# Latent attention: which engine copies the turned tiles out of PSUM

## The reference, cut to what matters

```python
s = (einsum('bqhd,bkhd->bhqk', qn_b, k_nope) + einsum('bqhd,bkd->bhqk', qr_b, k_rope)) * scale
s = where(causal, s, -inf)
p = softmax(s, axis=-1)
o = einsum('bhqk,bkhd->bqhd', p, v)
```

## Time and profile before

| | |
|---|---|
| median of 3 runs | 2243.24 us (2241.24 to 2244.13) |
| the profiled execution | 2243.0 us, of which the span from first to last instruction is 2241.2 us |
| mean granted TensorE clock | 0.957 of full |
| busy: PE, PEld | 2107.5 us (94%), 1801.6 us (80%) |
| busy: DVE, ACT, POOL | 830.4 (37%), 740.2 (33%), 776.8 us (35%) |
| chain that ended last | PE 86%, issue 4%, DVE 4%, ACT 2% |

### The profile page before, as it was taken

How to read it: one execution, slowest core, us unless ns; L and a number is a source line. 1 busy time by engine, 2 the same in 40 slices (tenths; PEclk the granted TensorE clock), 3 DMA queues, 4 the chain that set the end, 5 groups by cost and what they waited for, 6 DMA issues and landing times.

```text
span 2241.2 us, 32733 instructions
## 1 busy us (share of the span) xinstructions
PE 2107.5 (94%) x14312; PEld 1801.6 (80%) x14312; DVE 830.4 (37%) x1293; ACT 740.2 (33%) x1093; POOL 776.8 (35%) x244
## 2 busy tenths in 40 slices
PE   7999999979988889999999789989999899999998
PEld 5898888859766679999998677977777688888886
DVE  3400674053456643211222411654445554211222
ACT  5332223245546433221223243322111433221222
POOL 4443333444321344334433200343222444434432
PEclk9999999989989999999999777989999999999999
DMA  4222212222301122223224000211111422323322
GB/s 163 94 95 90 71 66 76 94 66 89 97 22 38 38 76 76 86 80 100 95 71 119 28 30 1 63 57 40 59 40 48 143 94 93 94 85 104 94 77 73
DMA packets 170982, 169.47 MB, mean 76 GB/s; under 512 B 16844, under 2 KB 164680, under 8 KB 170840
## 3 DMA queue, kind: packets, MB, share of 16 engines
q1 hardware_dynamic: 169436, 165.15, 23.4%
q10 hardware_dynamic: 1404, 2.23, 0.3%
HBM read 162.12 MB, written 5.24 MB: 75 GB/s over the span
## 4 chain that ended last, share of the span: by engine, by line
PE 86%; issue 4%; DVE 4%; ACT 2%; POOL 2%; DMA 1%; ACTq 0%; SPq 0%; DVEq 0%; POOLq 0%
PE ps L1927 84%; PE ps L1929 2%; POOL w_lo L687 1%; POOL residual L710 1%; ACT w_hi L812 0%; ACT diag L840 0%; DMA x_rows<-in_x 0%; POOL stat L704 0%; DVE sumsq L1263 0%; DVE tmp L1694 0%; DVE mla_out_lo L1882 0%; POOL gdn_small L759 0%; POOL gdn_small L757 0%; DVE gdn_on L1873 0%; DVE mla_k L1620 0%
## 5 line engine op out<-in xcount | busy, mean ns | idle before, releaser
L687 POOL TENSOR_TENSOR w_lo<-w_raw,w_hi 128x2048 fp32r<-128x2048 f32 (+3 forms) x157 | 675.4, 4305 | 903.8 <-ACT w_hi L812 903.8
L1927 PE MATMUL ps<-u_hi,w_hi 128*128 128x512 f32 (+1 forms) x1904 | 597.1, 353 | 32.5 <-DVE sg L1466 12.3
L1927 PE MATMUL ps<-u_lo,w_hi 128*128 128x512 f32 (+1 forms) x1904 | 587.3, 348 | 0.0
L1927 PE MATMUL ps<-u_hi,w_lo 128*128 128x512 f32 (+1 forms) x1904 | 586.0, 348 | 0.0
L1927 PEld LDWEIGHTS ps<-u_hi,w_hi 128*128 128x128 f32 x1904 | 335.6, 192 | 82.3 <-issue 20.6
L1927 PEld LDWEIGHTS ps<-u_hi,w_lo 128*128 128x128 f32 x1904 | 334.3, 192 | 43.2 <-issue 0.7
L1927 PEld LDWEIGHTS ps<-u_lo,w_hi 128*128 128x128 f32 x1904 | 334.7, 192 | 39.9 <-issue 1.2
L812 ACT ACTIVATE w_hi<-w_raw 128x2048 fp32r<-128x2048 f32 (+3 forms) x157 | 279.6, 1783 | 182.2 <-PE ps L1927 172.8
L1927 PE MATMUL ps<-hidden_hi,w_hi 128*128 128x264 f32 (+1 forms) x528 | 141.1, 321 | 0.0
L1927 PE MATMUL ps<-hidden_lo,w_hi 128*128 128x264 f32 (+1 forms) x528 | 141.0, 322 | 0.0
L1927 PE MATMUL ps<-hidden_hi,w_lo 128*128 128x264 f32 (+1 forms) x528 | 140.8, 321 | 0.0
(11 more groups left out here) (380 smaller groups left out, 3050.1 us busy)
## 6 DMA issues: line engine op xcount, KB each, us to landing
w_raw<-in_w_in_a SPq DMA_DIRECT2D x23, 1024.0 KB, 5.2
w_raw<-in_ffn_w_gate SPq DMA_DIRECT2D x22, 1024.0 KB, 5.3
w_raw<-in_ffn_w_up SPq DMA_DIRECT2D x22, 1024.0 KB, 5.3
w_raw<-in_w_in SPq DMA_DIRECT2D x17, 1024.0 KB, 5.2
w_raw<-in_ffn_w_down SPq DMA_DIRECT2D x16, 768.0 KB, 4.6
w_raw<-in_ffn_w_down SPq DMA_DIRECT2D x16, 640.0 KB, 4.0
w_raw<-in_w_out_a SPq DMA_DIRECT2D x8, 1024.0 KB, 5.1
w_raw<-in_w_kv SPq DMA_DIRECT2D x8, 1024.0 KB, 5.6
```

The costliest lines, as they stand in the source:

```text
L687: pool.tensor_tensor(WL[:, u % RAWS, part], RAW[:, u % RAWS, part], WH[:, u % SPLITS, part].bitcast(F32), ALU.subtract).then_inc(lo_done, 1)
L1927: return nc.tensor.matmul(o, a, b, start=start, stop=stop, **kw)
```

## The change

The copies of turned items and turned pairs leave ACT's loop and enter DVE's, in the same step, after the row maximum and ahead of the reciprocal and the product for a finished head. Waits, buffers and counts are the same. ACT keeps the exponents and their sums.

```diff
@@ ACT's loop over steps @@
-                for kind, g in mla_step_turns(s):
-                    no = mla_turn_no[kind, g]
-                    act.wait_ge(ma_t, no + 1)
-                    if kind == "item":
-                        b = g % NT
-                        if g >= 2:
-                            act.wait_ge(ma_pv, g - 1)
-                        if b < NT - 1:
-                            n = P * (b + 2)
-                            nc.scalar.activation(MPT[:, g % 2, 0:n], PS[:, 4 + no % 2, 0:n], ACT.Copy).then_inc(ma_pt, 1)
-                        else:
-                            nc.scalar.activation(MPT[:, g % 2, 0:SEQ], PS[:, 4 + no % 2, :], ACT.Copy)
-                            nc.scalar.activation(MPT[0:META, g % 2, SEQ:640], PS[0:META, 7, 0:P],
-                                                 ACT.Copy).then_inc(ma_pt, 1)
-                    else:
-                        nc.scalar.activation(OMF[:, g, :], PS[:, 4 + no % 2, :], ACT.Copy).then_inc(ma_pt, 1)
@@ DVE's loop over steps, between the maximum and the norm @@
+                for kind, g in mla_step_turns(s):
+                    no = mla_turn_no[kind, g]
+                    dve.wait_ge(ma_t, no + 1)
+                    if kind == "item":
+                        b = g % NT
+                        if g >= 2:
+                            dve.wait_ge(ma_pv, g - 1)
+                        if b < NT - 1:
+                            n = P * (b + 2)
+                            nc.vector.tensor_copy(MPT[:, g % 2, 0:n], PS[:, 4 + no % 2, 0:n]).then_inc(ma_pt, 1)
+                        else:
+                            nc.vector.tensor_copy(MPT[:, g % 2, 0:SEQ], PS[:, 4 + no % 2, :])
+                            nc.vector.tensor_copy(MPT[0:META, g % 2, SEQ:640], PS[0:META, 7, 0:P]).then_inc(ma_pt, 1)
+                    else:
+                        nc.vector.tensor_copy(OMF[:, g, :], PS[:, 4 + no % 2, :]).then_inc(ma_pt, 1)
                 if s >= 7 and (s - 7) % NT == 0 and (s - 7) // NT < HEADS:
                     h = (s - 7) // NT
```

## The result

| | before | after |
|---|---|---|
| median of the first comparison | 2242.24 us (4 runs, 2237.4 to 2244.1) | 2262.72 us (4 runs, 2260.0 to 2269.2) |
| span of the profiled execution | 2241.2 us | 2258.1 us |
| latent attention's loop | 112.3 us | 129.7 us |
| PE's waits at seven heads' ends | 7.2 us | 10.0 us |
| granted clock in the loop | 0.73 | 0.62 |

The ratio is 1.0099 with a 95% interval of 1.0072 to 1.0126: the kernel became slower by 20 us, where +5.2 us was forecast and the range ended at 2258. The direction and the place were right, the size wasn't.

A forecast was written before the change was run, and what follows sets the result against it. PE was taken to bound the kernel, its wait for DVE's finished-head product being the one to watch. Terms of +3.5, -0.2, +0.2 and +1.7 us for the clock gave +5.2 us, 2248.2 us, range 2241 to 2258.

The forecast's parts named there:

- What bounds the loop: Latent attention's loop: PE bounds it, and its 7.2 us of waits for DVE's finished-head product are the ones to watch.
- The copy inside the wait: At seven heads' ends a 384-wide copy on DVE delays reciprocal and product, 0.50 us each, +3.5 us.
- The copies that left ACT: Copies come earlier than behind ACT's exponents; only a ramp wait of PE could gain, -0.2 us.
- the exponents: ACT's exponents start no earlier, and copies on DVE delay no maximum: 0, at most +1.2 us.
- the drain: At the loop's end, the last pair's copy and item 31's copies take longer by DVE: +0.2 us.
- Rival D: ACT's chain of exponent and copy limits the loop, so the move gains: 2241.5 us at best; 0.05 together with another rival.
- The clock: half a fall more: Longer idle at heads' ends makes TensorE's clock fall more often in the loop; half a 6.8 us fall, +1.7 us.
- bound of -6.5 us: Lower bound of the clock term: the first two whole heads run like the later ones of 13.9 us.
- rival C: The loop's clock returns earlier, its 40.8 us at half clock cut to 6.8: 2239.6 us; chance 0.13.
- B: Rival: the clock locks low, two or more heads staying at half clock, 4.8 us each: 2256 us; chance 0.15.
- A: Rival: PE's wait at heads' ends grows but the clock doesn't react: +3.5 us, 2246.5 us; chance 0.25.
- E: Rival: PE's wait at heads' ends doesn't grow, something other than DVE's queue binding: 2243 us; 0.05 together with another rival.

The follow-up runs named there:

- norm_first: The kernel before with reciprocal and product for a finished head moved ahead of the row maximum, copies still on ACT: 2208.8 us, ratio 0.9876.
- copy_after_norm: The changed kernel with reciprocal and product for a finished head put ahead of the copies in DVE's loop: 2239.0 us, ratio 0.9996.
- after_again: The changed kernel run once more unedited, beside the kernel before on one chip: 2263.7 us, ratio 1.0153.

## Why the prediction was wrong

- *What bounds the loop.* Right. PE's wait for L1665 was the one wait that mattered, and DVE's queue the one that the change lengthened.
- *The copy inside the wait: 0.50 us each, 3.5 us.* Right: 0.46 us at full clock and 0.49 at half, the 384-wide copy 552 ns for an expected 548. In sum 10.0 us instead of 7.2, 2.8 and not 3.5, because four of the seven waits now fall into half clock instead of two, and each is shorter there. The Trainium skill's estimate of 525 ns for this copy ("VectorE: DVE Perf Modes", "The TRN2 errata") is 5% under the measured 552.
- *The copies that left ACT, the exponents, the drain: about nothing.* Right for this kernel; no maximum stood behind a copy, and the copies' earlier end served nobody. The profile's view of waits now names the copy L1647 as releaser of 12.6 us at PE's weight loads; these are the same seven waits, put down to the semaphore that came before the last. Rival D, that the copies were the limit, is false here and true in small once the wait is gone: 0.33 us a head, as norm_first shows, 2.6 us of the loop. The Trainium skill's rule to empty PSUM with both ScalarE and VectorE ("TensorEngine Tiling (Array Packing)", "PSUM Bottleneck") isn't tested by that: in both kernels both engines read PSUM, maxima on one and exponents on the other, and only the copies' place differs.
- *The clock: half a fall more, +1.7 us.* Wrong, and this is the step that failed. The term measured 14.6 us in the two traces. I counted falls and gave each the 6.8 us of the last three; the number of falls even went down, from four to three in the loop, but they lasted 23.9, 27.3 and 48.5 us up to the loop's end. The row that said so was in hand: the first fall of the kernel before lasted 40.8 us. I took it for the exception, and the later ones for the pattern. The second trace of the kernel before has both as well, two of 6.8 us behind one of 23.9; with the longer wait the short ones are gone. The prediction's last sign of being wrong, a clock in this loop far from 0.73 that moves the time by more than the copies do, is what came. (The bound of -6.5 us and rival C's -6.9 are one sum, which gives -6.8; nothing hangs on it.)
- *The rivals.* The outcome is B, which had 0.15, and its price for the clock, two heads at 4.8 us, was two thirds of the 14.6 measured. A, the longer wait at an unchanged clock, had 0.25; at most two of the changed kernel's ten runs, 2248 and 2253 us on the last chip, fit it. copy_after_norm has E's case, a wait that doesn't grow, and E's time. C's way, an early return of the clock, is by its times what the kernel before itself does in its lower group; none of the changed kernel's ten runs did it.
- *The range.* My bound for the clock was +19 us, which with the other terms is 2265.5; the measured median lies inside that bound, and the range cut it off at 2258. No row of the kernel before gave a ground for cutting there.

## What to carry to other kernels

Before an instruction is put into an engine's list, ask which release stands behind it in that list and whether TensorE waits for that release: here the block's place, not its engine, decided between no change and +20 us, and moving the release ahead of the independent work gave -31 us. Where the granted clock of a stretch is neither 1.00 nor 0.50 on average, a short, regular idle time of TensorE may be what holds it there; as the range of a change of that idle time take the gap between the stretch at full and at half clock (here loops of 83.5 and 138.9 us), not the idle time itself, and try to take the idle time away first.

## What the runs showed of the hardware

In this loop TensorE's clock stayed at 2.4 GHz with seven idle times of 0.9 us, 10.1 to 10.5 us apart, and fell to 1.2 GHz in every traced kernel that had them at 1.1 us or more: after 11 of 18 such ends of heads at 1.1 to 1.2 us, after 16 of 16 at 1.3 us or more. Once down it came back after anything from 6.8 us to 44 us inside a loop, and in after_again not at all in the 123 us that were left of it, though PE was busy for 114 of them. Making the waits at full clock 0.2 us shorter (the first one 0.3) moved the median from 2239.8 to 2213.7 us. A kernel at that edge has two groups of times, some 30 us apart, with no change of program. What in PE's work, beside the idle time, decides when the clock returns (one stretch of 41 us and three of 6.8 in one loop) the runs don't settle.
